# Banks for the turned rows, one-request stores and the order of work on the engines in a hybrid encoder layer

## The reference

```
h  = x @ w_in                         -> q | k | v | u, 512 columns each
A  = stick-breaking attention(q, k, v)   8 heads x 64, strictly causal
     log_1m = log(1 - sigmoid(z)) where key < query; after = reverse cumulative sum
     a = exp(log_sigmoid(z) + after);  out = a @ v
B  = for 4 groups of 128 columns of u, windows 2, 4, 8, 16:
     (trailing mean - token) @ pool_w[g] * pool_scale
x1 = LayerNorm(ALPHA * x + concat[A, B] @ w_out)
y  = LayerNorm(ALPHA * x1 + (silu(x1 @ w_gate) * (x1 @ w_up)) @ w_down)      D_FF = 2816
```

## Time and profile before

| | us |
|---|---|
| median of 3 runs | 2558.46 |
| lowest and highest | 2557.19, 2559.26 |
| the profiled execution | 2559.62 |
| its span | 2557.8 |
| PE busy | 2502.2 (98%) |
| DVE, ACT, POOL busy | 1573.8, 1157.1, 1171.4 |

### The profile page before, as it was taken

One profiled execution on the slowest core, in us unless ns is written; L12 is line 12 of the kernel. 1 busy time (PEld: TensorE's weight loads), 2 busy tenths in 40 slices (PEclk: granted clock), 3 DMA queues, 4 the chain that ended last, 5 costly groups with the idle time before them and its releaser, 6 DMA issues.

```text
span 2557.8 us, 37203 instructions
## 1 busy us (share of the span) xinstructions
PE 2502.2 (98%) x13846; PEld 2136.3 (84%) x13846; DVE 1573.8 (62%) x2127; ACT 1157.1 (45%) x1940; POOL 1171.4 (46%) x1016
## 2 busy tenths in 40 slices
PE   9999999999999999999999999999999999999998
PEld 9978898788778978787888887878878887899997
DVE  3265246576644367887644577887774355866776
ACT  4465326664422155665522255656553214433333
POOL 5475427744323155565522274556643114344434
PEclk9999999999999999999999999999999999999999
DMA  8887846653345233333363233333523512233322
GB/s 244 261 253 242 310 160 200 189 174 108 112 139 199 80 124 123 113 122 106 95 233 134 83 115 104 120 104 103 169 79 136 192 59 98 91 93 114 97 93 85
DMA packets 189715, 361.67 MB, mean 141 GB/s; under 512 B 34432, under 2 KB 86272, under 8 KB 189536
## 3 DMA queue, kind: packets, MB, share of 16 engines
q1 hardware_dynamic: 189536, 359.30, 43.6%
HBM read 297.44 MB, written 61.80 MB: 140 GB/s over the span
## 4 chain that ended last, share of the span: by engine, by line
PE 83%; DVE 6%; issue 3%; POOL 3%; ACT 2%; DMA 2%; SPq 0%; DVEq 0%; POOLq 0%; ACTq 0%
PE bank L1361 26%; PE bank L1423 19%; PE bank L1312 9%; PE bank L1267 7%; PE bank L1369 7%; PE bank L1161 5%; PE bank L1212 4%; PE bank L1177 4%; DVE left L2005 1%; DMA gw_lo_raw<-in_w_in_dram 1%; POOL gw_lo L2687 1%; DVE acc L2043 1%; POOL beta L2617 1%; PE bank L1289 1%; DVE stats L2025 0%
## 5 line engine op out<-in xcount | busy, mean ns | idle before, releaser
L1361 PE MATMUL bank<-x1T,gw_hi 128*128 128x512 f32 (+1 forms) x2336 | 711.7, 388 | 3.7 <-DVE hT_lo_raw L2135 2.3
L2617 POOL TENSOR_TENSOR beta<-beta,left 128x512 f32<-128x512 f32 (+2 forms) x326 | 354.8, 1089 | 367.2 <-DVE left L2005 366.8
L1361 PEld LDWEIGHTS bank<-x1T,gw_hi 128*128 128x128 f32 x2336 | 418.4, 188 | 84.3 <-issue 3.7
L1361 PE MATMUL bank<-x1T,gw_lo 128*128 128x512 f32 (+1 forms) x1168 | 447.8, 383 | 0.0
L2644 POOL TENSOR_TENSOR gw_lo<-gw_lo_raw,gw_hi 128x1024 fp32r<-128x1024 f32 x70 | 182.5, 2608 | 441.8 <-ACT gw_hi L1633 441.6
L1538 ACT ACTIVATE aT<-bank 128x512 fp32r<-128x512 f32 (+2 forms) x326 | 173.7, 533 | 438.7 <-PE bank L1177 390.3
L1312 PE MATMUL bank<-x1T,gw_hi 128*128 128x256 f32 (+2 forms) x1472 | 353.8, 332 | 5.6 <-DVE first_qk L2341 2.0
L2316 DVE TENSOR_TENSOR acc<-bank,acc 128x512 f32<-128x512 f32 x312 | 213.6, 687 | 204.5 <-PE bank L1423 201.1
L1990 DVE TENSOR_TENSOR aT<-bank,aT 128x512 fp32r<-128x512 f32 (+2 forms) x326 | 197.3, 605 | 194.9 <-ACT aT L1538 193.4
L1423 PE MATMUL bank<-dw_hi,hT_hi 128*128 128x512 f32 x728 | 295.4, 406 | 9.8 <-issue 5.8
L1423 PE MATMUL bank<-dw_lo,hT_hi 128*128 128x512 f32 x728 | 286.5, 394 | 0.0
(11 more groups left out here) (223 smaller groups left out, 4584.8 us busy)
## 6 DMA issues: line engine op xcount, KB each, us to landing
gw_lo_raw<-in_w_gate_dram SPq DMA_DIRECT2D x88, 512.0 KB, 3.6
gw_lo_raw<-in_w_up_dram SPq DMA_DIRECT2D x88, 512.0 KB, 3.6
dw_lo_raw<-in_w_down_dram SPq DMA_DIRECT2D x86, 512.0 KB, 4.4
gw_lo_raw<-in_w_in_dram SPq DMA_DIRECT2D x64, 512.0 KB, 4.8
k_st<-kT_scratch SPq DMA_DIRECT2D x80, 256.0 KB, 4.1
v_st<-v_scratch SPq DMA_DIRECT2D x80, 256.0 KB, 4.3
mixT<-mixT_scratch SPq DMA_DIRECT2D x32, 512.0 KB, 6.1
acc<-in_xT_prompt_dram SPq DMA_DIRECT2D x16, 512.0 KB, 6.4
```

Of the source, the lines that this page charges most:

```text
L1361: m = pe.matmul(gu_bank(g, n)[:, 0:w], gw[L % 4][a][:, k, :], x1T[x][:, k, first:first + w], start=k == 0 and s == 0, stop=k == KD - 1 and ...
L2617: pool.tensor_tensor(x[:, 0:w], x[:, 0:w], left[n % RL][:, 1:w + 1], ALU.mult).then_inc(a_done, 1)
```

## The change

- **Banks.** `t_at` gives the bank of each turn. Items with an odd number in their block whose turn comes before slot 246 (`side`) now turn into bank 3, all others into bank 6 as before; `t_prev` is the item that last used the same bank. The first of `side` also waits for `wop_moved`, the first `turn_x` for the last of `side`.
- **Scratch layout and stores.** The sample's 32 columns lie behind block 0's 512, and the later blocks are 32 columns further on. Block 0's keys and queries are stored by one request per head instead of two.
- **Turns to the last block.** They use banks 4 and 5 or 6 and 7 in turn instead of 0 and 1; two come ahead of the first down products, the others one step ahead of where they were, and each waits for the split of the one before the last.
- **Order on DVE.** `hidden_lo` comes ahead of the background of its slot; in the last pair before the seven-product form, the sum `S_3` and `gate_quarters_lo(0)` change places with `extra_lo(0)`.
- **Order on POOL.** `ladder_step` ahead of `weights_lo` in a slot; in block 2's last pair the last slot's `up_lo` ahead of the background.

```diff
@@ -409,7 +409,7 @@
             use_of[n] = len(stored_before[u]) - 1
-            requests = 2 * (2 if n < 16 else 1)
+            requests = 2
             stored_before[u].append(stored_before[u][-1] + 16 * requests)
...
@@ -509,16 +509,13 @@
     z_ring = {b: [4, 5] for b in range(BLOCKS)}
-    t_ring = {b: [6] for b in range(BLOCKS)}
     z_at, z_prev, t_at, t_prev = [], [], [], []
...
         k = n - BASE[it.block]
-        for ring, places, prevs, users in ((z_ring[it.block], z_at, z_prev, z_user),
-                                           (t_ring[it.block], t_at, t_prev, t_user)):
-            places.append(ring[k % len(ring)])
-            prevs.append(users.get(places[-1]))
-            users[places[-1]] = n
+        z_at.append(z_ring[it.block][k % 2])
+        z_prev.append(z_user.get(z_at[-1]))
+        z_user[z_at[-1]] = n
 
...
@@ -533,6 +530,12 @@
         return ITEMS[n].sample and not ITEMS[n].first
+
+    DECODE = slice(BW, XW)
+
+    def columns_at(b):
+
+        return slice(b * BW + (DEC if b else 0), (b + 1) * BW + (DEC if b else 0))
 
...
@@ -681,6 +684,13 @@
 
+    turn_slot = {BASE[b] + s - AT_TURN: slot for slot, ticks in due.items() for kind, b, s in ticks if kind == ATTENTION}
+    side = [n for n in range(N) if turn_slot[n] < FP - 10 and (n - BASE[ITEMS[n].block]) % 2]
+    for n in range(N):
+        t_at.append(D_BANK + 1 if n in side else T_BANK)
+        t_prev.append(t_user.get(t_at[-1]))
+        t_user[t_at[-1]] = n
+
     def chunks(b):
...
@@ -703,6 +713,11 @@
     WINO_CHUNKS = 2 * (PAIRS - WINO_FROM)
+
+    def x_bank(b, t):
+        if b == 0:
+            return D_BANK
+        return GU_BANK if b < BLOCKS - 1 else Z_BANK if t % 2 == 0 else T_BANK
 
...
@@ -787,12 +802,12 @@
                 if not it.sample:
-                    dst = mixT_d[:, it.head * HD:(it.head + 1) * HD, it.block * BW:(it.block + 1) * BW]
+                    dst = mixT_d[:, it.head * HD:(it.head + 1) * HD, columns_at(it.block)]
                     sp.dma_start(r32(dst.rearrange("j r t -> r j t")), r32(o_both[rows_for(g), :, :]))\
...
                 for j, part in enumerate((o_hi, o_lo)):
-                    dst = mixT_d[j, it.head * HD:(it.head + 4) * HD, SEQ:TOK].rearrange("(h d) t -> d h t", h=4)
+                    dst = mixT_d[j, it.head * HD:(it.head + 4) * HD, DECODE].rearrange("(h d) t -> d h t", h=4)
                     src = part[rows_for(g), 0:4 * DEC].rearrange("d (h t) -> d h t", h=4)
...
@@ -973,9 +988,8 @@
             def store_pair(n, dst, rows):
                 b, u = n // 16, pair_of(n)
-                sp.dma_start(r32(dst[:, :, b * BW:(b + 1) * BW]), r32(both[b][u][rows, :, 0:BW])).then_inc(parts_stored[u], 16)
-                if b == 0:
-                    sp.dma_start(r32(dst[:, :, SEQ:TOK]), r32(both[b][u][rows, :, BW:XW])).then_inc(parts_stored[u], 16)
+                to = slice(0, XW) if b == 0 else columns_at(b)
+                sp.dma_start(r32(dst[:, :, to]), r32(both[b][u][rows, :, :])).then_inc(parts_stored[u], 16)
 
             def store_keys_or_queries(n):
...
@@ -1165,6 +1179,8 @@
                 pe.wait_ge(a_done, it.macro + it.size)
+                if u == side[0]:
+                    pe.wait_ge(wop_moved, 8)
                 if t_prev[u] is not None:
...
@@ -1280,13 +1296,19 @@
                 pe.wait_ge(shifted, ln_tiles[ln_index(1, b)] + t + 1)
-                if b:
+                if b == BLOCKS - 1 and t == 0:
+                    pe.wait_ge(m_added, mix_count(BLOCKS))
+                elif b == BLOCKS - 1 and t == 1:
+                    pe.wait_ge(aT_lo, N)
+                    pe.wait_ge(o_sum, len(group_last))
+                elif b:
                     pe.wait_ge(prod, 2 * PAIRS * b)
...
                     pe.wait_ge(p_vlo, 4 * BLOCKS)
-                pe.wait_ge(x_lo, XP + BT * b + t)
+                    pe.wait_ge(aT_lo, side[-1] + 1)
+                pe.wait_ge(x_lo, XP + BT * b + t - (1 if b == BLOCKS - 1 and t else 0))
                 for k in range(KD):
-                    m = pe.transpose(bank[(GU_BANK if b else D_BANK) + k // 4][:, (k % 4) * P:(k % 4 + 1) * P],
+                    m = pe.transpose(bank[x_bank(b, t) + k // 4][:, (k % 4) * P:(k % 4 + 1) * P],
                                      tile(b, t)[:, k * P:(k + 1) * P], ident[:, :])
...
@@ -1505,11 +1527,15 @@
                     background(next(slot))
-                    if d % 2 == 0:
-                        turn_x(b + 1, d // 2)
+                    if b < BLOCKS - 2:
+                        if d % 2 == 0:
+                            turn_x(b + 1, d // 2)
+                    elif d == 0:
+                        turn_x(b + 1, 0)
+                        turn_x(b + 1, 1)
+                    elif d % 2 == 0:
+                        turn_x(b + 1, d // 2 + 1)
                     downs(b, PAIRS - 1, d)
-                    if d == 2 * BT - 2 and tiles_of(b + 1) > BT:
-                        turn_x(b + 1, BT)
 
...
@@ -2474,13 +2500,14 @@
                         if pair == 0 and i == 2:
                             turned_lo(XP + 3, D_BANK, 3)
-                        now = ahead(next(slot))
+                        this = next(slot)
+                        if i == 2 and p:
+                            hidden_lo(b, p - 1, 1)
+                        now = ahead(this)
                         if i == 1 and before_wino:
                             token_sum(6)
                         if i == 0 and p:
                             times_up(b, p - 1, 1)
-                        if i == 2 and p:
-                            hidden_lo(b, p - 1, 1)
                         if i == 3:
                             gate_lo(4 * pair + 2)
...
@@ -2521,14 +2548,13 @@
                         now = ahead(next(slot))
                         if i == 0 and before_wino:
-                            extra_lo(0)
+                            quarter_sums(0, (S_3,))
+                            gate_quarters_lo(0)
                         if i == 1:
                             times_gate(b, p, 1)
                         behind(now)
-                        if i == 1 and before_wino:
-                            quarter_sums(0, (S_3,))
                         if i == 2 and before_wino:
-                            gate_quarters_lo(0)
+                            extra_lo(0)
                         second_norm(b, p, 3, i)
                         if i in (0, 3) and b == BLOCKS - 1 and p == 0:
...
@@ -2728,11 +2754,11 @@
                     S = PS * b + s
                     background(next(slot))
-                    if S in split_at and not by_vector(split_at[S]):
-                        weights_lo(split_at[S])
                     for x in range(4):
                         if S - x in done_at and place(done_at[S - x])[1] == POOLED:
                             ladder_step(done_at[S - x], x)
+                    if S in split_at and not by_vector(split_at[S]):
+                        weights_lo(split_at[S])
                     if S - 1 in WOP_AT:
                         out_pooled_lo(WOP_AT.index(S - 1))
...
@@ -2751,9 +2777,12 @@
                     for i in range(4):
+                        weights_first = pair == PAIRS * (BLOCKS - 1) - 1 and i == 3
+                        if weights_first:
+                            up_lo(4 * pair + 3)
                         background(next(slot))
                         second_norm(b, p, 1, i)
-                        if i == 3:
+                        if i == 3 and not weights_first:
                             up_lo(4 * pair + 3)
...
```

24 lines of the change are left out of this document (12 added, 12 removed).

## The result

The kernel after takes 2542.10 us (median of 6 runs, 2539.77 to 2543.19) against 2558.86 us before (6 runs, 2557.19 to 2562.27). The ratio is 0.9933, with an interval of 0.9920 to 0.9945: faster by 0.55% to 0.80%, more than the 0.2% that can be told from no change. Forecast were 2545.5 us and a range of 2540 to 2555 us. In a later comparison the same kernel took 2540.86 us (5 runs, 2539.64 to 2543.35). The profiled executions took 2559.62 us before and 2541.69 us after; the spans, 2557.8 and 2539.9 us, differ by 17.9 us.

The account below looks back on a forecast made before the run. PE is busy 2502.2 us of a 2557.8 us span, so only its waits can go. The parts sum to 14.0 us, less 1 us for shifted waits: 2558.5 - 13 = 2545.5 us, range 2540 to 2555 us.

Parts of the forecast that it names:

- Part 1: Two banks for the turned rows in the projections: PE's waits for the single bank go, 3.6 us gained.
- part 3: Block 0's stores in one request: the weight load behind them on SP's queue comes earlier, 1.3 us, bounds 0 and 2.0.
- part 4: hidden_lo ahead of slot 2's background on DVE: PE's waits ahead of the downs go, 3.5 us, bounds -5 and 5.
- a product or values that are ready follow: At 214.76 and 216.99 us PE meets no new wait behind the turns, so 1.86 us is gained.
- Next wait: Rival: what PE gains in the projections it waits for at the next scan; 2551 us, chance 0.24.
- Part 2: Ladder step ahead of weights_lo on POOL: scores near 490 us come earlier, 2.2 us, bounds 0 and 2.2.
- "nothing" for the later weights: With the ladder step first, weights come 1.3 us later, four slots ahead of their use: no cost.
- deduction of 1.0 us: Taken off for hidden_lo delaying aT and the scan, and for gate_lo coming ahead of POOL's beta.
- DVE's queue: Rival: hidden_lo pays 0.67 us into the turn-score loop in 31 pairs, +20.8 us; 2565 us, chance 0.04.
- Part 5: Block 2's last pair, up_lo ahead of the norm's last rows on POOL: 1.4 us, bounds 1.0 and 1.6.
- part 6: Last turns run while hT_lo is made, and two pairs of banks alternate: 2.0 us, bounds 1.2 and 2.3.
- Part 7: Sums before the seven-product pairs reordered: the 1.99 us wait goes, others replace it; 0, bounds -0.8 and 1.5 us.

Follow-up runs that it names:

- experiment 8: Kernel after with each GpSimd subtraction for the weights' lower parts (weights_lo) issued as two halves of 128x512: 2542.23 us, ratio 0.9932.
- experiments 3 and 4: 3: kernel before with the two banks for turned rows alone, 2556.74 us; 4: kernel after with weights_lo ahead of the ladder's steps again, 2545.32 us.
- experiment 1: Kernel after with block 0's keys and queries stored by two requests again: 2543.68 us, ratio 0.9944.
- experiment 2: Kernel before with 16 transposes of 128 columns ahead of block 1's first product, filling PE's wait there: 2557.98 us, ratio 0.9998.
- experiment 5: Kernel before with hidden_lo ahead of the background of its slot on DVE and nothing else: 2554.17 us, ratio 0.9980.
- experiment 7: Kernel after with the last sums in their old order, plus 16 transposes on PE during the wait there: 2542.57 us, ratio 0.9935.

## Why the prediction came out as it did

The gain lies where the prediction had put it and the signs of the parts held; the sum was 3.4 us short of the median. Part 1 and the requests of part 3 gave less than their terms, part 4 and the clock more, so that the total is closer than its terms are.

- **Part 1 (3.6, measured 2.9).** Two steps were off. I had read the three waits that the list puts down to POOL's beta as waits for the bank, like the one of the earlier trace rows. At 464.91 us that was false: the last beta of this macro itself ends last, behind weights_lo, and a wait of 0.75 us is still there. At 214 us the bank's wait went as forecast, but the values behind it waited 1.18 us for aT, since DVE's difference is held by weights_lo (experiment 8) or, in the old order, by the ladder step. The step "a product or values that are ready follow" failed there for 0.9 us of 1.9. "Next wait" was right for this place, not for the whole.
- **Part 2 (2.2, measured 2.3)** held, with its condition that both edits are needed (experiments 3 and 4) and its row for who gets SBUF first. Its "nothing" for the later weights failed in block 0, where PE waits for them at 87 us and loses 0.7 us; it is luck that the start at 114 us, which hangs on a load, swallows this.
- **Part 3 (1.3, measured 0.9 at the start and 1.5 by the clock).** The start at 114 us came 0.9 us earlier, but the requests are worth 0.45 us of that (experiment 1): the term was mis-sized, since it took 0.65 us off for each request left out, while the two that remain in the same stretch now take 1.98 us on the queue, where the four took 2.6. The rest is not shown to be the edit's. What I missed is the clock: I priced the wait of 2.00 us at its length, while the trace before also has 3.4 us at half clock at its end, 1.5 us more. The windows of that stretch show it (experiment 2); the list of waits, on which I priced it, does not.
- **Part 4 (3.5, measured 6.0)** is the term that was mis-sized most. The 4.5 us of waits were right. The deduction of 1.0 us was not needed: neither turns nor scores wait longer (experiment 5). And what comes on top of a wait's length, which I left as a reserve at 0.1 to 0.2 us, was 0.24 us at each of six places, 1.5 us. The rival "DVE's queue" asked for 20.8 us more; nothing of it is there.
- **Part 5 (1.4, measured 1.7) and part 6 (2.0, measured 1.9)** held; the excess of part 5 is again what comes on top of a wait.
- **Part 7 (0, measured 0.0)** held, and for the reason given: the 1.99 us of the earlier trace rows came back as 0.51, 0.46 and 1.22 us. What it may be worth lies outside the sum: no stretch at half clock stands behind the three short waits in any trace, and one stands behind the long one in two of the five traces that have it.

The rival "next wait" adds parts 4 to 6 to 6.5 us where their terms make 6.9; it doesn't change its reading.

What the sum as a whole lacked is what a removed wait gives beyond its length, and the clock. Together they account for most of the 5.4 us by which PE is less busy: 1.5 us are the one stretch at half clock (three products of 256 columns start in 0.64 us there and in 0.35 us otherwise), and thirteen waits fewer in the list make 3.1 us at 0.24 us each, an estimate from experiment 5. For the medians the clock counts more than for these two profiles: over the fifty runs of the kernel before that were timed beside the experiments the mean granted clock is 0.9980, over the eleven of the kernel after 0.9992. At 0.0007 for one stretch that is between one and two stretches fewer per run, by this estimate 2 to 3 us of the 16.8 us by which the median fell.

## What to carry to other kernels

On an engine that is 98% busy a removed wait was worth its length and about 0.24 us more here, and a long one may hide a stretch at half clock behind it: read the granted clock in windows right behind each long wait before pricing it. A wait that the list puts down to one releaser has to be checked against the last instruction of each of its inputs, and then the next instruction asked for what it would wait for at the earlier time. Where two engines exclude each other, the one that starts first decides, so move the short instruction ahead of the long one, or cut the long one only where something short stands behind it. A load's arrival in one profile does not price an edit on its queue; the time from one issue to the next on that queue does.

## What the runs showed that I had not expected

**The clock.** In the 14 profiled executions PE waits 14 times for 1.9 to 2.5 us (the wait ahead of its first instruction left aside). Behind ten of these waits the granted clock is at half for 3.4 us, beginning between 0.4 us before and 1.5 us behind the wait's end; behind four it is not, and the same wait (2.23 us at 494 us) is of both kinds in two executions. Apart from the program's last microseconds no stretch at half clock stands anywhere else, and none follows the 52 waits of 1.4 to 1.8 us. By its end each has cost 1.4 to 1.6 us, of which a later wait can give back a part (experiment 7). The kernel after, which has no wait that long left, has no such stretch in either of its traces.

**Contention.** A DVE instruction with two inputs in SBUF takes 0.69 us if it starts 0.1 us ahead of POOL's 128x1024 subtraction and 2.77 us if it starts 0.2 us behind it; POOL then takes 2.85 us in the first case and 2.40 in the second. With 512 columns in POOL's instruction DVE is held for 1.66 us in all. The Trainium skill's GPSIMD Engine Reference (Key points) says that the two contend for such operands; the runs agree, and in them the one that starts second pays. So in this kernel DVE and POOL meet not only at semaphores.

**Spread of a load.** The weight load ahead of block 1's first product came between 105.9 and 109.3 us in the 14 traces, far more than the 0.45 us that the second requests are worth.
